# A chunked RWKV-7 recurrence on one NeuronCore: gram matrices, diagonal blocks and exp(growth) issued in another order around a group's inverse, with signs and end decays moved from VectorE to ScalarE

## The reference, cut to what matters

```python
def rwkv7_step(S, inp):
    r, w, k, v, a, b = inp                     # a = -kk, b = iclr * kk
    sa = jnp.einsum('dbhvk,dbhk->dbhv', S, a)
    S = S * w[..., None, :] + sa[..., None] * b[..., None, :] + v[..., :, None] * k[..., None, :]
    y = jnp.einsum('dbhvk,dbhk->dbhv', S, r)
    return S, y
```

## Time and profile before

| | us |
|---|---|
| median of 3 runs | 3053.94 |
| lowest and highest of them | 3052.82, 3054.43 |
| the profiled execution, its time | 3051.29 |
| its span in the trace | 3049.5 |

### The profile page before, as it was taken

The page is one execution under the profiler, slowest core; times in us unless marked ns, Lnnn a source line. Parts: engine busy times, 40 slices in busy tenths (PEclk is TensorE's granted clock), DMA queues, the critical chain, the costliest instruction groups (busy, mean ns, idle before and its releaser), DMA issues. The chain is left out here.

```text
span 3049.5 us, 54624 instructions
## 1 busy us (share of the span) xinstructions
PE 2724.9 (89%) x20770; PEld 2152.9 (71%) x20770; DVE 2072.2 (68%) x3096; ACT 1360.0 (45%) x2618; POOL 652.3 (21%) x779
## 2 busy tenths in 40 slices
PE   7889989998737788896899789999799999799999
PEld 4655578884437788784667678888588888588887
DVE  6867723235566676645446778888888888587786
ACT  4547711116624455453244434545444454344443
POOL 5447700000025788741332000000000000000000
PEclk9999999999968899998999899999899999899999
DMA  4442233324775445335654222222122221726401
GB/s 131 145 97 50 49 80 70 74 55 156 287 207 160 125 129 135 96 100 174 194 168 145 80 103 83 77 83 81 54 83 80 83 76 66 276 100 223 160 29 55
DMA packets 309627, 352.37 MB, mean 116 GB/s; under 512 B 123049, under 2 KB 213673, under 8 KB 309250
## 3 DMA queue, kind: packets, MB, share of 16 engines
q1 hardware_dynamic: 304482, 343.63, 35.9%
q10 hardware_dynamic: 4896, 5.38, 0.5%
HBM read 245.77 MB, written 103.14 MB: 114 GB/s over the span
## 5 line engine op out<-in xcount | busy, mean ns | idle before, releaser
L99 PE MATMUL up_p<-up_b_hi,up_a_hi 128*128 128x512 f32 x1232 | 491.3, 399 | 43.6 <-ACT inv L2303 22.1
L100 PE MATMUL up_p<-up_b_lo,up_a_hi 128*128 128x512 f32 x1232 | 490.8, 398 | 0.0
L101 PE MATMUL up_p<-up_b_hi,up_a_lo 128*128 128x512 f32 x1232 | 490.3, 398 | 0.0
L99 PEld LDWEIGHTS up_p<-up_b_hi,up_a_hi 128*128 128x128 f32 x1232 | 234.1, 190 | 103.9 <-ACT inv L2303 23.4
L100 PEld LDWEIGHTS up_p<-up_b_lo,up_a_hi 128*128 128x128 f32 x1232 | 234.3, 190 | 56.2
L101 PEld LDWEIGHTS up_p<-up_b_hi,up_a_lo 128*128 128x128 f32 x1232 | 233.9, 190 | 55.7
L2746 ACT CAST down_a_hi<-down_a 128x512 fp32r<-128x512 f32 x154 | 96.0, 623 | 260.5 <-PE down_p_x L101 142.6
L2258 ACT CAST up_a_hi<-up_a_sum 128x512 fp32r<-128x512 f32 x132 | 81.4, 617 | 224.5 <-DVE up_a_sum L2417 145.7
L2761 DVE TENSOR_TENSOR down_a_lo<-down_a,down_a_hi 128x512 fp32r<-128x512 f32 x154 | 106.4, 691 | 98.4 <-ACT down_a_hi L2746 98.4
L2328 ACT ACTIVATE up_con<-up_raw,vecs_sb 128x1023 f32<-128x1023 f32 (+1 forms) x88 | 109.7, 1246 | 128.3 <-DVE up_raw L2487 84.2
L2493 DVE SCALAR_TENSOR_TENSOR up_con<-up_raw,vecs_sb,up_con 128x1023 f32<-128x1023 f32 (+1 forms) x88 | 113.0, 1284 | 66.5 <-ACT up_con L2328 66.5
(11 more groups left out here) (292 smaller groups left out, 6980.1 us busy)
## 6 DMA issues: line engine op xcount, KB each, us to landing
up_a_raw<-in_w_up SPq DMA_DIRECT2D x172, 256.0 KB, 2.8
down_a<-in_w_down SPq DMA_DIRECT2D x88, 256.0 KB, 8.7
down_b<-act_out SPq DMA_DIRECT2D x88, 256.0 KB, 9.1
rec_inp<-gate_chunks SPq DMA_DIRECT2D x64, 256.0 KB, 3.4
rec_inp<-gate_chunks SPq DMA_DIRECT2D x256, 64.0 KB, 2.8
first_w<-in_w_attn SPq DMA_DIRECT2D x24, 512.0 KB, 3.5
rkv_chunks<-rwkv_project_mix SPq DMA_DIRECT2D x12, 1024.0 KB, 6.5
gate_chunks<-gates_out SPq DMA_DIRECT2D x3, 4096.0 KB, 12.2
```

The lines of the kernel that those rows point to most:

```text
L99: pe.matmul(out, w_hi, x_hi, start=start, stop=False, skip_group_check=True)
L100: pe.matmul(out, w_hi, x_lo, start=False, stop=False, skip_group_check=True)
L101: return pe.matmul(out, w_lo, x_hi, start=False, stop=stop, skip_group_check=True)
```

## The change

The number of matmuls, transposes and copies stays. What changes:

- PE: `gram` of the front chunk is issued right behind `h_part`, ahead of `y_part`, `tok_part` and `cross`; before, it stood between `cross` and `corner`.
- ACT: `gram_copy` stands behind `decay` and ahead of `y_copy`; `growth` behind `y_copy`, and thus ahead of the boundary's `spread` and of `tok_copy`.
- DVE: in a boundary slot `turn_back` stands behind `state`, `state_decay`, `diagonal_a`, `diagonal_b` and directly ahead of `turn`.
- kk is no longer negated: `scaled` is one tensor_tensor in place of a scalar_tensor_tensor with -1, the diagonals are taken with a mask of -1 (`minus_halves`, two more columns of masks), and `u_copy` and `gram_copy` multiply by -1 on their way.
- `dec_end` is written by ACT as its own exponential of 128x4 per direction; the DVE copy of 128x4 goes.

```diff
-MASK_COLS = dict(halves=2, both0=128, both1=128, running0=128, running1=128)
+MASK_COLS = dict(halves=2, minus_halves=2, both0=128, both1=128, running0=128, running1=128)
...
                                          (now and c > 0, y_state, c), (now and c < NCH - 1, h_part, c),
-                                         (now, y_part, c), (ahead, tok_part, c + 1),
-                                         (ahead, cross, c + 1), (front, gram, c + LAG),
-                                         (ahead, corner, c + 1)):
+                                         (front, gram, c + LAG), (now, y_part, c), (ahead, tok_part, c + 1),
+                                         (ahead, cross, c + 1), (ahead, corner, c + 1)):
...
-                    copy(stacked[d][HALVES[0], c % 2, :, 1], bank[d][0][HALVES[0], :, 0:L])
-                    copy(stacked[d][HALVES[1], c % 2, :, 0], bank[d][0][HALVES[1], :, 0:L]).then_inc(
-                        S["u_copied"][d], 1)
+                    for h, rows in enumerate(HALVES):
+                        op = nc.scalar.activation(stacked[d][rows, c % 2, :, 1 - h], bank[d][0][rows, :, 0:L], ACT.Copy,
+                                                  scale=-1.0)
+                    op.then_inc(S["u_copied"][d], 1)
...
-                    nc.scalar.activation(dec[d][:, :, 1:L + 1], given(d, f, "csum"), ACT.Exp,
-                                         scale=-KAPPA).then_inc(S["dec"][d], 1)
+                    csum = given(d, f, "csum")
+                    nc.scalar.activation(dec_end[d][:, f], csum[:, :, (0 if d else L - 1)], ACT.Exp, scale=-KAPPA)
+                    nc.scalar.activation(dec[d][:, :, 1:L + 1], csum, ACT.Exp, scale=-KAPPA).then_inc(S["dec"][d], 1)
...
-                    copy(ring_g[d][:, f % RING, :, BL:L], bank[d][2][:, :, BL:L]).then_inc(S["g_copied"][d], 1)
+                    nc.scalar.activation(ring_g[d][:, f % RING, :, BL:L], bank[d][2][:, :, BL:L], ACT.Copy,
+                                         scale=-1.0).then_inc(S["g_copied"][d], 1)
...
-                                         (after, decay, c + LAG + 1), (now, y_copy, c),
+                                         (after, decay, c + LAG + 1), (front, gram_copy, c + LAG),
+                                         (now, y_copy, c), (after, growth, c + LAG + 1),
                                          (ahead and fresh, spread, c + 1), (ahead, tok_copy, c + 1),
-                                         (after, growth, c + LAG + 1), (ahead, cross_copy, c + 1),
-                                         (front, gram_copy, c + LAG)):
+                                         (ahead, cross_copy, c + 1)):
...
-                    nc.vector.scalar_tensor_tensor(out=ar[d][:, f % RING, :, 0:L], in0=given(d, f, "kk"),
-                                                   scalar=-1.0, in1=dec[d][:, :, 2 * d:2 * d + L],
-                                                   op0=ALU.mult, op1=ALU.mult)
-                    end = 1 if d else L
-                    nc.vector.tensor_copy(dec_end[d][:, f], dec[d][:, :, end])
+                    tt(ar[d][:, f % RING, :, 0:L], given(d, f, "kk"), dec[d][:, :, 2 * d:2 * d + L], ALU.mult)
...
-                    if ahead and (c + 1) % GROUP == 0:
-                        turn_back((c + 1) // GROUP)
                     for go, stage, n in ((carry, state, c), (carry, state_decay, c),
                                          (front, diagonal_a, c + LAG), (front, diagonal_b, c + LAG)):
                         if go:
                             for d in DIRS:
                                 stage(n, d)
+                    if ahead and (c + 1) % GROUP == 0:
+                        turn_back((c + 1) // GROUP)
```

More of the change, by code:

```diff
@@ L57, in host_constants @@
         ident=p == q, heads_ones=same, all_ones=np.ones((128, 128)),
-        halves=np.concatenate([s < 32, s >= 32], 1),
+        halves=np.concatenate([s < 32, s >= 32], 1), minus_halves=-1.0 * np.concatenate([s < 32, s >= 32], 1),
         both0=np.concatenate([s < t, s <= t], 1), both1=np.concatenate([s > t, s >= t], 1),
@@ L1552, in _ @@
                 tt = nc.vector.tensor_tensor
-                half = lambda j: mask_of("halves")[:, j:j + 1]
+                minus_half = lambda j: mask_of("minus_halves")[:, j:j + 1]
                 STEPS = 2 * (BL - 1)
@@ L1603, in diagonal_a @@
                     done_all(dve, "turned", f // GROUP)
-                    nc.vector.tensor_scalar(E[:, problems(f, d)], bank[d][2][:, :, 0:BL], half(0), None,
+                    nc.vector.tensor_scalar(E[:, problems(f, d)], bank[d][2][:, :, 0:BL], minus_half(0), None,
                                             ALU.mult).then_inc(S["diag_a"][d], 1)
@@ L1609, in diagonal_b @@
                     at = problems(f, d)
-                    nc.vector.scalar_tensor_tensor(out=E[:, at], in0=bank[d][2][:, :, BL:L], scalar=half(1),
+                    nc.vector.scalar_tensor_tensor(out=E[:, at], in0=bank[d][2][:, :, BL:L], scalar=minus_half(1),
                                                    in1=E[:, at], op0=ALU.mult, op1=ALU.add).then_inc(
```

## The result

| | us |
|---|---|
| median of 10 runs, the changed kernel | 3066.94 (3062.85 to 3072.5) |
| median of 10 runs, the kernel before | 3053.99 (3048.8 to 3061.01) |
| ratio, 95% interval | 1.0045 [1.0034, 1.0056] |
| the profiled execution after, its time and span | 3072.5, 3070.7 |

What follows compares the result with a forecast made beforehand. POOL's loop, 58.3 us per group, bounds the kernel; the other loop becomes 53.45 + 4.3 + 0.7 + 2.6 - 0.8 = 60.25. Five periods give +9.8, first and last group +1.2 each: sum +12, median 3066 us, range 3044 to 3074.

Steps and rivals of the forecast that it cites:

- the other loop: Work of the engines other than POOL over one group: 53.45 us before, forecast 60.25 after.
- 4.85 of slack: DVE's average boundary wait for POOL: the other engines' work is ready 4.85 us sooner per group.
- Two loops, and which is the longer: Per group, POOL's loop sets 58.3 us before; after, the other loop's 60.25 exceeds POOL's 52.4.
- Middle slot, +1.4 us, to 13.7: Middle slots: y_copy and cross_copy behind gram_copy on ACT delay corner and x_part by 1.4 us, three per group, +4.3.
- state and diagonals ahead of turn_back, +2.6 and +0.7: Boundary slot: turn_back waits for state, state_decay and diagonals, +2.6 us; state waits for h_part, +0.7.
- Less in the way behind returned, -0.8: Boundary, behind returned: growth gone ahead of cross_copy and gram ahead of corner gain 0.8 us per group.
- growth no longer waited for: Boundary: growth stands ahead of spread, so POOL's 6.93 us wait for it goes.
- First and last group, +1.2 each: First group has a lighter slot 0, last only turn_back behind state: +1.2 us put on each.
- Arithmetic at nothing: End decays on ACT are hidden under state and diagonals; dropping DVE's copies changes nothing if the other loop decides.
- Rival 1: Faster: ACT's row does not delay corner, middle slots stay at 12.3 us, 3040 us; chance 0.14.

Runs made afterwards that it cites:

- e9: The changed kernel run once more, unaltered: 3064.69 us, ratio 1.0039 to the kernel before.
- e12: The changed kernel with its new order in middle slots only, boundary slots in the order of before: 3050.55 us, ratio 1.0002 to before.
- e4: The changed kernel with ACT's old order in middle slots, gram still early on PE: 3051.33 us, ratio 0.9995 to before.
- e3: The changed kernel with its new PE and ACT order in boundary slots only: 3052.88 us, ratio 1.0005 to before.
- e5: The changed kernel with DVE's old order (turn_back first), middle slots as before, gram_copy last in boundary slots: 3034.74 us, ratio 0.9950 to before.
- e1: The changed kernel with the old stage orders on PE, ACT and DVE, keeping only the new arithmetic: 3053.38 us, ratio 1.0002 to before.
- e8: The kernel before with all four order edits of e6, keeping the old arithmetic: 3031.44 us, ratio 0.9935 to before.
- the filler: The changed kernel with tok_part's transposes issued twice in middle slots holding a front chunk: 3062.02 us, repeated 3065.28 us.
- e6: As e5, but at the boundary DVE takes turn_back, diagonals, turn, then state and state_decay: 3028.79 us, ratio 0.9924 to before.

## Why the prediction was right

The time, 3066.94 us, lies by the 3066 forecast. The mechanism holds: the work moved ahead of turn_back and the longer middle slots made the other loop the longer one. That the number is hit so closely is in part luck, since errors of opposite sign cancel. Per group, the forecast adds 4.3 for middle slots, 3.3 ahead of turn_back and -0.8 behind it, and takes off 4.85 of slack: 1.95. The traces give 2.9, 3.4, +0.3 and 4.57: 2.05. In e9's trace, taken in an execution of 3064.24 us, groups grew by 1.5 us only, and the last group's 3.7 made up for it. Step by step:

- **Two loops, and which is the longer.** Right. POOL decided before (in e12 the other loop used up some 4.2 us more per group at no cost in time), the other loop decides after (no wait for POOL in any boundary slot). Forecast 60.25 us per group, measured 60.43; POOL's own step from turn to solve is 2.08 us (forecast 2.1).
- **Middle slot, +1.4 us, to 13.7.** Right in mechanism (e4 undoes it by ScalarE's row alone), too large in size. The slots take 13.34 to 13.44 us in the group without a low-clock stretch, and 13.62 in the mean of all 15, as forecast; but the forecast started from a single slot of 12.30 us. The ten distances between middle slots before take 12.61 in the mean, so the difference is +1.0, and +0.8 against the 12.79 of e3 and e4. Two things inside were not foreseen. In four of the five groups POOL waits for growth while one slot's state_decay runs, and the pair then takes 0.75 us in place of 1.3 (the row at 1139.79, against 1.38 at 1152.57 where POOL works): such slots take 12.8. And in those same groups one slot takes 14.9 to 15.7 with a stretch at the lower clock.
- **state and diagonals ahead of turn_back, +2.6 and +0.7.** Measured 2.55 and 0.86: the one term right in mechanism and size, and by e3 and e5, which lie 0.55% apart, the decisive one.
- **Less in the way behind returned, -0.8.** Wrong; it is +0.3. The first state follows turn_back by 17.0 us in the mean of five groups, 16.7 before. At the boundary of the rows, corner does start 6.8 us behind turn_back in place of 8.2, and x_part 8.6 in place of 9.6. But the slow stretch does not end sooner: here it lasts to 13 us behind turn_back, before to 10, and falls on other matmuls. pairs_part starts 12.2 us behind turn_back, 11.6 before, and takes 2.70 us in place of 2.06. First the changed kernel (matmuls, then the clock), then the kernel before:

```profile
1128.43 1.07 PE L1304 MATMUL rec_bank<-rec_Z,rec_low 64*64 64x32 f32 x16
...
1133.74 2.70 PE L1381 MATMUL rec_bank<-rec_ar,rec_bk 64*128 64x128 f32 x32
```

```profile
1125.00:1135.00 10.00, 8.51 (x140) 8.26 (x142) 5.19 (x8) 3.98 (x12) 8.05 (x19) 0.50 0.30 84
```

```profile
1122.95 2.06 PE L1381 MATMUL rec_bank<-rec_ar,rec_bk 64*128 64x128 f32 x32
```

- **growth no longer waited for.** Wrong in the row: POOL still waits 5.90 us for it at the boundary, since growth sits behind the boundary's diagonals and POOL has long ended its solve. It costs nothing: keys ends at 1125.42, and the next solve waits for turn, which ends at 1127.17.

```profile
1122.91 2.51 POOL L1537 TENSOR_TENSOR rec_bk<-rec_inp,rec_grow 128x512 f32<-128x512 f32 x2 [5.90 <-ACT rec_grow L1470]
```

- **First and last group, +1.2 each.** Wrong in both, and no row stood behind the 1.2. The first is unchanged (58.16 against 58.10), the last +4.15 (55.36 against 51.21), of which about 2.4 us are state and state_decay ahead of turn_back (from mask's end); the changed kernel's second trace, e9, has +3.7.
- **Arithmetic at nothing.** Right (e1, e8). The Trainium skill (ScalarE: Activation LUTs, What ACT_TABLE_LOAD costs) gives 186 ns plus 0.833 ns per element for an ACTIVATE with immediate scale and bias, by which I estimate 189 ns for an end decay of 128x4; the 195 ns measured here agree.

Rival 1 named the true prize, a loop that loses nothing in the middle slots, but e3 shows that it is not enough: as long as state and the diagonals precede turn_back, the other loop takes 57.65 us. The order that wins is one that neither the change nor my forecast contained.

The lower clock is shown by the granted clock of the rows. That TensorE's short waits bring it about is supported, not shown. For it: the traces of e3 and e4 show no such stretch (e3's TensorE waits in a middle slot for rec_ys alone, up to 1.0 us, e4's for rec_low alone, up to 0.5; the changed kernel's for both in one slot), and the filler removed it. Against it: the same two waits (0.40 to 0.56 us for rec_ys, 0.52 to 0.70 for rec_low) stand in each of the three middle slots of the changed kernel's group from 1182 us, which has no stretch, and e12, with both waits too, has a stretch in two groups of five. So the two waits are not enough by themselves, and what decides is open. That the stretch costs time in the end is not shown either, since the filler left the time where it was.

## What to carry to other kernels

When two loops feed each other, measure both: 4.85 us of slack per period can be spent once. The changed kernel spent it in the middle slots and again at the hand-over, each free by itself (e12, e3) and 13 us together. A single slot or a single wait is a poor base for such a sum: take the mean over the periods that count. At a hand-over to the engine that sets the pace, place first what releases that engine (turn_back), next what it needs to go on (diagonals, turn), and last what only the next slot needs (state): e6, 0.76% faster than the kernel before with no work removed.

## What the runs showed of the hardware

- With TensorE's waits of 0.45 and 0.70 us in a slot of otherwise dense small matmuls, the granted clock fell to 0.5 for 3 to 4 us in the middle of three of the five groups in e9 and four in the first trace of the changed kernel, without any single long wait; the slot that it hits is some 2 us longer. The other groups have the same waits and no stretch. The kernel before has a wait of 0.46 us in the same slots and no stretch either.
- Moving matmuls out of a slow stretch after a long wait saved nothing here: the stretch took the next ones (pairs_part 2.70 us in place of 2.06, the first state 17.0 us behind turn_back in place of 16.7).
- state_decay, a VectorE instruction with two inputs in SBUF, takes 0.75 us per pair while GpSimd rests and 1.38 in the row at 1152.57 of the changed kernel, where it works. Where the new order makes GpSimd wait, VectorE's pair is the shorter.
